# Warm-up products on ones, an earlier first k-tile, and norm vectors on another queue in a fused decoder trunk

## What is computed

```
h    = rmsnorm(x, norm_mix_g)                  # x: 256 x 2048
proj = h @ w_in                                # 2048 x 8192: q, k, v of 8 + 8 heads, and a gate
lam  = exp(sum(lambda_q1*lambda_k1)) - exp(sum(lambda_q2*lambda_k2)) + lam_init
d    = rmsnorm(diff_attention(q, k, v, lam), subln_g) * (1 - lam_init)     # 8 heads
m    = moba_attention(q, k, v)                                             # 8 heads, one block at this length
x    = x + (concat(d, m) * silu(gate)) @ w_out
h2, mn = rmsnorm(x, norm_mem_g), rmsnorm(mem, mem_norm_g)
x    = x + softmax(h2 @ w_q_mem . km) vm @ w_o_mem                         # km, vm = mn @ w_kv_mem
out  = rmsnorm(x, final_g)
```

## Time and profile before

| what | value |
|---|---|
| median of 3 executions | 573.56 us (573.34 to 574.38) |
| the profiled execution's own time | 572.92 us |
| its span, first to last instruction | 571.1 us |
| mean granted TensorE clock | 0.996 |
| TensorE matmul busy | 562.1 us (98%) |
| VectorE, ScalarE busy | 425.9 us (75%), 406.6 us (71%) |
| instructions | 8602 |

### The profile page before, as it was taken

The page is one execution under the profiler, slowest core; times in us unless marked ns, Lnnn a source line. Parts: engine busy times, 40 slices in busy tenths (PEclk is TensorE's granted clock), DMA queues, the critical chain, the costliest instruction groups (busy, mean ns, idle before and its releaser), DMA issues.

```text
span 571.1 us, 8602 instructions
## 1 busy us (share of the span) xinstructions
PE 562.1 (98%) x2640; PEld 468.0 (82%) x2640; DVE 425.9 (75%) x716; ACT 406.6 (71%) x651; POOL 2.1 (0%) x26
## 2 busy tenths in 40 slices
PE   8999999999999999999999999999999999999994
PEld 7888888888888888888888888888888888888884
DVE  4769769678886877866756768668568886877975
ACT  5786866967868778776784784875598786855543
POOL 1000000000000000000000000000000000000000
PEclk9999999999999999999999999999999999999998
DMA  8997769568676776886875976779799986983803
GB/s 272 353 280 238 210 173 250 169 201 230 190 233 192 200 216 188 234 224 163 250 215 157 264 199 192 220 194 299 246 229 266 260 248 187 260 230 111 244 2 147
DMA packets 151236, 123.32 MB, mean 216 GB/s; under 512 B 66809, under 2 KB 133162, under 8 KB 150698
## 3 DMA queue, kind: packets, MB, share of 16 engines
q1 hardware_dynamic: 151112, 122.98, 76.3%
q10 hardware_dynamic: 98, 0.03, 0.0%
HBM read 105.93 MB, written 2.10 MB: 189 GB/s over the span
## 4 chain that ended last, share of the span: by engine, by line
PE 98%; DVE 1%; ACT 0%; POOL 0%; issue 0%; ACTq 0%; POOLq 0%
PE ps L614 28%; PE ps L615 28%; PE ps L616 28%; PE ps L697 2%; PE ps L650 1%; PE ps L654 1%; PE ps L658 1%; PE ps L679 1%; PE ps L850 1%; PE ps L855 1%; PE ps L851 1%; PE ps L637 1%; PE ps L772 1%; PE ps L624 0%; PE ps L818 0%; PE ps L682 0%
## 5 line engine op out<-in xcount | busy, mean ns | idle before, releaser
L1209 DVE TENSOR_TENSOR w_lo<-w_raw,w_hi 128x1024 fp32r<-128x1024 f32 x183 | 222.5, 1222 | 106.2 <-ACT w_hi L880 104.2
L880 ACT ACTIVATE w_hi<-w_raw 128x1024 fp32r<-128x1024 f32 x183 | 192.6, 1057 | 82.3 <-PE ps L616 81.3
L614 PE MATMUL ps<-w_hi,aT 128*128 128x512 f32 x540 | 211.8, 392 | 0.0
L615 PE MATMUL ps<-w_lo,aT 128*128 128x512 f32 x540 | 210.3, 389 | 0.0
L616 PE MATMUL ps<-w_hi,aT 128*128 128x512 f32 x540 | 210.1, 389 | 0.0
L616 PEld LDWEIGHTS ps<-w_hi,aT 128*128 128x128 f32 x540 | 101.4, 188 | 21.2
L614 PEld LDWEIGHTS ps<-w_hi,aT 128*128 128x128 f32 x540 | 101.4, 188 | 21.0
L615 PEld LDWEIGHTS ps<-w_lo,aT 128*128 128x128 f32 x540 | 101.4, 188 | 20.4
L614 PE MATMUL ps<-w_hi,yT_hi 128*128 128x512 f32 x144 | 56.2, 390 | 0.0
L616 PE MATMUL ps<-w_hi,yT_lo 128*128 128x512 f32 x144 | 56.0, 389 | 0.0
L615 PE MATMUL ps<-w_lo,yT_hi 128*128 128x512 f32 x144 | 56.0, 389 | 0.0
(11 more groups left out here) (202 smaller groups left out, 569.1 us busy)
## 6 DMA issues: line engine op xcount, KB each, us to landing
w_raw<-in_w_in SPq DMA_DIRECT2D x251, 256.0 KB, 3.2
w_raw<-in_w_out SPq DMA_DIRECT2D x64, 256.0 KB, 4.0
w_raw<-in_w_kv_mem SPq DMA_DIRECT2D x32, 256.0 KB, 4.5
w_raw<-in_w_q_mem SPq DMA_DIRECT2D x16, 256.0 KB, 3.0
w_raw<-in_w_o_mem SPq DMA_DIRECT2D x16, 256.0 KB, 3.8
mems<-in_mem SPq DMA_DIRECT2D x1, 2048.0 KB, 10.1
xs<-in_x SPq DMA_DIRECT2D x3, 512.0 KB, 6.3
w_raw<-in_w_in SPq DMA_DIRECT2D x10, 128.0 KB, 5.5
```

The costliest lines, as they stand in the source:

```text
L614: pe.matmul(acc, hi[:, k0 + k, tok], w_hi[:, slot, k], start=first and k == 0, stop=False)
L615: pe.matmul(acc, hi[:, k0 + k, tok], w_lo[:, slot, k], start=False, stop=False)
L880: act.activation(w_hi[:, i % SPLITS], raw, ACT.Copy).then_inc(hi_made, 1)
L1209: dve.tensor_tensor(lo, w_raw[:, i % RAW], hi.bitcast(F32), ALU.subtract).then_inc(lo_made, 1)
```

## The change

It does four things. The warm-up products take a 128 x 128 tile of ones (the first half of `r_row`), written by VectorE at the start, in place of the identity, and there are ten ahead of the gain's transposition and six behind x's in place of three and two. The turns of x's k-tiles 2 and 3 go inside k-tile 1, and those of 4 and 5 inside k-tile 3, between its second and third pair of products. The three norm vectors are issued by the sync queue behind the weights of half 2, and are turned behind k-tile 6. Lambda is spread by a product of 128 rows: the column is zeroed but for its first row.

```diff
-ROWS_BEHIND = {0: (2,), 1: (3,), 2: (4, 5), 4: (6, 7), 6: (8, 9, 10, 11), 10: (12, 13, 14, 15)}
+ROWS_AMID = {1: (2, 3), 3: (4, 5)}
+ROWS_BEHIND = {4: (6, 7), 6: (8, 9, 10, 11), 10: (12, 13, 14, 15)}
...
-WARM_UP = (3, 2)
+WARM_UP = (10, 6)
...
-        ones_row = sbuf("ones_row", [1, P])
...
+        ones = r_row[:, 0:P]
...
# sync queue
+                if n == 2:
+                    for row, vec in ((0, norm_mem_g), (KO, mem_norm_g)):
+                        sp.dma_start(gains[row:row + KO, :], vec[0].rearrange("(k p) -> k p", p=P)
+                                     ).then_inc(gains_loaded, 16)
+                    sp.dma_start(gains[2 * KO:2 * KO + 1, :], subln_g).then_inc(gains_loaded, 16)
...
# GpSimd
-            pool_e.memset(ones_row[:, :], 1.0).then_inc(ones_ready, 1)
...
# TensorE
                 with pe.Fori(0, count):
-                    pe.matmul(ps[:, 2, 0:P], ident[:, :], ident[:, :], start=True, stop=True)
+                    pe.matmul(ps[:, 2, 0:P], ones, ones, start=True, stop=True)
...
                     for t in range(NT):
                         pe.matmul(ps[:, t, :], aT_lo[:, k, t * P:(t + 1) * P], w_hi[:, slot, i],
                                   start=False, stop=False)
+                    for later in ROWS_AMID.get(k, ()):
+                        transpose_rows(later)
                     pe.wait_ge(k_lo if i == 0 and n < SINGLE else lo_made, n + 1)
...
-                    if k == 1:
+                    if k == 6:
                         transpose_gains()
...
-                            pe.wait_ge(ones_ready, 1)
                             pe.wait_ge(lam_ready, 2)
-                            pe.matmul(ps[:, 6, SEQ:SEQ + 1], ones_row[:, :], neg_lam_row[0:1, :], start=True, stop=True
+                            pe.matmul(ps[:, 6, SEQ:SEQ + 1], ones, neg_lam_row[:, :], start=True, stop=True
...
+            pe.wait_ge(ones_ready, 1)
+            keep_busy(WARM_UP[0])
             pe.wait_ge(ident_ready, 2)
-            keep_busy(WARM_UP[0])
             pe.wait_ge(mix_gain_loaded, 16)
...
# ScalarE
-            for row, vec in ((0, norm_mem_g), (KO, mem_norm_g)):
-                act.dma_start(gains[row:row + KO, :], vec[0].rearrange("(k p) -> k p", p=P)).then_inc(gains_loaded, 16)
-            act.dma_start(gains[2 * KO:2 * KO + 1, :], subln_g).then_inc(gains_loaded, 16)
...
# VectorE
+            dve.memset(ones, 1.0).then_inc(ones_ready, 1)
+            dve.memset(neg_lam_row, 0.0).then_inc(lam_zeroed, 1)
             dve.wait_ge(gainsT_made, 1)
...
                 if n == 9:
                     dve.wait_ge(lam_exps, 1)
+                    dve.wait_ge(lam_zeroed, 1)
```

More of the change, by code:

```diff
@@ L326, in program @@
         ones_ready = sem("ones_ready")
+        lam_zeroed = sem("lam_zeroed")
         lam_made = sem("lam_made")
```

## The result

The changed kernel takes 575.76 us (median of 6, 575.49 to 576.17) against 573.57 (median of 6, 573.25 to 574.47): a ratio of 1.0035, 95% interval 1.0022 to 1.0048. It is slower by 2.2 us. Its profiled execution took 575.69 us with a span of 573.9, which is 2.8 us more than the profiled one of before; that one lay 0.65 us under its own median. The forecast was 576.3.

The account below looks back on a forecast made before the run. TensorE, its matmuls busy for 98% of the span, was taken to bound the kernel, so start delays pass through almost whole. Warm-up 2.85 plus turns 0.62 gave 3.47 us on 572.92: 576.4, rounded 576.3, range 574.4 to 577.8.

Parts of the forecast that it names:

- The start of the warm-up: First warm-up load waits for one VectorE memset instead of GpSimd's identity: at 1.03 us, 0.67 earlier.
- Ten products for three: First warm-up loop at 0.45 us a turn: gain's load at 5.81 us, x's transpositions at 5.95 against 3.65.
- Six products for two: Second warm-up loop, between x's transpositions and k-tile 0: 2.45 us, k-tile 0 at 8.4 against 5.55, delay 2.85 us.
- twelve records 0.21 us apart: Second warm-up loop: records spaced like this would refute the forecast's cost of 0.40 to 0.45 us a turn.
- the estimate from it: Second loop's turn priced from the page's 108 ns branch: near the array's 0.21 us, result 0.7 us lower, 575.7.
- The turns of x: Inside k-tiles 1 and 3: two stalls of 0.71 us, less gains of 0.58 and 0.22, together +0.62 us.
- The norm vectors: Issued by the sync queue, turned behind k-tile 6: nothing in total; 0 to 0.5 us if the cover were gone.
- Lambda: Two records of 0.38 us together replaced by two with 128 rows: zero, 0.1 us either way.
- The sum: Whole kernel: 2.85 + 0.62 = 3.47 us on the profiled 572.92, giving 576.4, rounded 576.3.
- rivals with other mechanisms (574.7 and 575.2): Clock rises well inside the ten products: 574.7, chance 0.20; x's turns cost no more, only the warm-up counts: 575.2, chance 0.10.
- the cold end: Rival: low clock to the end of the warm-up, k-tile 0 at 9.35, 577.9 us, chance 0.10.
- the early rise: Rival: clock rises well inside the ten products, k-tile 0 at 6.7, 574.7 us; chance 0.20, half of it within 0.2%.

Follow-up runs that it names:

- row 2 early: Kernel before with five and two products on ones, lambda by 128 rows, row 2 turned behind k-tile 1's first pair: 572.66 us against 573.69, ratio 0.9985.

## Why the prediction was right, point by point

*The start of the warm-up* was put at 1.03 us; it was 1.13 in the chain, since VectorE began its memset at 0.84.

*Ten products for three:* x's transpositions were forecast for 5.95 and began at 6.00. The ten products took 4.66 us at the low clock, 0.47 each against the 0.45 of the sum, and the way from x's turns over ScalarE to k-tile 0, 7.7, was read rightly.

*Six products for two* is the step that failed. K-tile 0 was put at 8.4, by 2.45 us for six turns "issued from the moment the transpositions are", taken as 5.95, and it came at 7.7. The price was right: the sequencer spent 5.2 to 7.5 us in the loop, 0.4 us a turn, at either clock. The starting point was wrong by 0.8 us: the issue runs ahead of the array. The semaphores ahead of the second loop had long been raised, so its first turns were issued while the last of the ten slow products were still being worked off. Six turns from 5.2 end just when ScalarE is ready, so the forecast's sum counted time that had already passed. The prediction's own sign, twelve records 0.21 us apart, couldn't tell this: the records lay 0.11 apart, 0.22 a product, and would have refuted a price that was right. By the Trainium skill, "Advanced Engine Details and Errata", section "Control Flow Timing", a compare-and-branch takes about 108 ns, and the estimate from it, 575.7 us for the whole, lies next to the measured 575.76. That is luck. The sequencer's records give 0.215 us for a branch that is taken, twice the page's figure, and it wasn't a cheap turn that hid the loop, it was the lead.

*The turns of x* were put at +0.62, in the profile they cost 0.46, with both stalls at their places and released by ScalarE's high part. Alone they cost more, 1.31 at the median, as the gains that I set against them (0.58 for a warm first pair, 0.22 at x's second part) belong to the warm-up. With these moved over, the forecast had 1.42 for the turns, near the 1.31, and 2.05 for the warm-up. That measured 1.5 in the profile, the difference being the six products, and 0.85 at the median, as the executions of before differ in how cold they start.

*The norm vectors* were put at nothing and cost 0.36 in the profile: the old place behind k-tile 1 gives nothing back, because k-tile 2 waits there for ScalarE anyway. I wrote that most of the time to landing was a queue of transfers, not the issue. For half 3, of which I wrote it, that was right: its first weights landed no later. For half 6 it was wrong: issued later, it landed at 22.0 in place of 20.6. In the changed kernel nothing waited for it, because TensorE was 3 us late itself; with a TensorE that was early 0.96 us were lost, more than the 0.5 that I gave.

*Lambda* was put at zero and gave 0.26 to 0.28 us back.

*The sum* by these: 2.13 + 0.46 + 0.36 - 0.26 = 2.7 us in the profile, where I had 3.47; 0.7 of the difference is the six products. The median moved by 2.2 only, since the profiled execution of before was 0.65 us faster than its median, which I had left out with the argument that a warm k-tile 0 would gain it back. That argument held. The forecast of 576.3 came within 0.5 us through errors that partly cancelled: 0.7 too much for the six products and 0.16 for the turns, 0.36 too little for the norm vectors, 0.26 too much for lambda. The range, 3.4 us wide, also held rivals with other mechanisms (574.7 and 575.2), so the time alone doesn't confirm this one; the rows do. Two slips changed little: the cold end takes 0.85 us for four transpositions that the earlier trace rows gives as 1.11, and half of the early rise is a chance of 0.10, not the 0.15 given for "within 0.2%".

## What to carry to other kernels

A long warm-up narrows the spread of the times and pays with a later start: it is free only as long as it ends before the first data lands. A loop's price is that of its issue, counted from when the sequencer enters it, which can be well before the array gets there. When a turn of operands is moved closer to its reader, count the work behind it against the chain of the other engine (here 1.4 us against 0.9), not against the wait that it avoids. And price an issue on a transfer queue by what is queued behind it: the next transfers may land as before (half 3), later ones need not (half 6), and that shows as soon as the reader gets faster.

## What the runs showed of the hardware

- The moment when TensorE's clock rises differs between executions of the same program. Seen by the durations, pairs took 0.85 us until 8.8 in the profile of the changed kernel with three products, and the pair from 6.43 took 0.45 in that of row 2 early with five; with ten, the twenty records took 4.66 us in one profile and 4.17 in another. The single times of the kernel before spread over 572.6 to 575.1; with ten and six products the spread was 0.6 to 0.7 us.
- The granted clock of the windows view reads 1.00 from the start, also where pairs take twice their time; before the first rise only the durations tell.
- A loop of one product costs 0.4 us a turn in issue, at either clock; its taken branch takes 0.215 us. The sequencer entered the second loop 0.8 us before the array began x's transpositions, and so hid part of it; with 24 products the array had caught up after about eight.
- With ten and six products k-tile 0 started at 7.66 to 7.71 us in three executions, though the ten products had ended up to 0.24 us apart: the issue of the sixteen turns, over at 7.5 in all three, keeps it there. That is a second reason, beside the clock, for the narrow spread; how much each gives is not shown.
- Three more issues on the sync queue ahead of half 3 did not make its first weights land later: 12.4 to 12.8 us in the seven profiles with them, 12.6 to 13.3 in the seven without. Half 6 landed at 21.1 to 22.6 with them and at 20.6 to 21.3 without.
- A product of one row by 128 columns, with the 512-column product behind it, took 0.74 us; with all 128 rows 0.46 us.
